# Moving a constants table behind the split rows, so that they begin at another offset within 512 bytes

## What is computed

```
# block 1: Fourier and convolution mixer, then 16 experts, each taking 32 tokens
h  = modulate(rms_norm(x));  p = h @ w_in                      # 1024 -> 5632
y_a = real(fft2(u_f)) @ w_fourier;  y_b = (b_g * conv3(c_g * v)) @ w_conv_out
x  = x + gate * ((sig(g_a) * y_a + sig(g_b) * y_b) @ w_o)
x  = x + gate * sum_over_experts(vals * (silu(xe @ w_gate) * (xe @ w_up)) @ w_down)
# block 2: two kinds of attention side by side
proj = rms_norm(x) @ w_in_2;  o_a = nsa_attention(...);  o_b = moba_attention(...)
x  = x + rms_norm((sig(.) * (o_a @ w_a) + sig(.) * (o_b @ w_b)) @ w_o)
# block 3: two layers, four kinds of attention and a gated feed-forward part
for l in 0, 1:
    proj = rms_norm(x) @ w_in_3[l];  x = x + concat(four attentions) @ w_o_3[l]
    h = rms_norm(x);  x = x + (silu(h @ w_gate) * (h @ w_up)) @ w_down
out = rms_norm(x)
```

## The kernel before

| tile | before | after |
|---|---|---|
| ring, x | 0 | 0 |
| cst | 0 | 256 |
| vec1 | 64 | 0 |
| vec2 | 0 | 448 |
| stat | 320 | 320 |
| xR | 320 | 256 |
| mt2, arena | 320 | 320 |

## Time and profile before

### The profile page before, as it was taken

How to read it: one execution, slowest core, us unless ns; L and a number is a source line. 1 busy time by engine, 2 the same in 40 slices (tenths; PEclk the granted TensorE clock), 3 DMA queues, 4 the chain that set the end, 5 groups by cost and what they waited for, 6 DMA issues and landing times.

```text
span 2136.2 us, 32653 instructions
## 1 busy us (share of the span) xinstructions
PE 1709.5 (80%) x13430; PEld 1239.9 (58%) x13430; DVE 808.7 (38%) x1592; ACT 646.8 (30%) x1144; POOL 84.0 (4%) x143
## 2 busy tenths in 40 slices
PE   5999966566556566665665799988999999999998
PEld 3899921112111222111121699988989988989996
DVE  2374621001110111110011557775656654666654
ACT  3334310000000000000000347655644334655333
POOL 2000010000000000000000200101100001000000
PEclk8999987877888787878778799999989999999999
DMA  9996799999999999999999753407065535145640
GB/s 368 328 323 231 284 380 428 429 428 428 428 430 428 428 429 428 428 428 430 428 428 430 274 187 120 139 33 269 21 213 182 196 138 184 40 159 170 195 178 20
DMA packets 152995, 613.51 MB, mean 287 GB/s; under 512 B 8816, under 2 KB 62138, under 8 KB 128312
## 3 DMA queue, kind: packets, MB, share of 16 engines
q1 hardware_dynamic: 148928, 604.47, 71.9%
q0 software_dynamic: 3200, 7.14, 1.1%
q10 hardware_dynamic: 760, 0.39, 0.1%
HBM read 610.88 MB, written 5.03 MB: 288 GB/s over the span
## 4 chain that ended last, share of the span: by engine, by line
PE 54%; DMA 38%; DVE 3%; ACT 2%; issue 1%; SPq 1%; DVEq 1%; POOL 0%; POOLq 0%; ACTq 0%
PE psum L1472 52%; DMA ring<-in_w_down_e 19%; DMA ring<-in_w_up_e 18%; DMA ring<-in_w_in 1%; PE psum L1842 1%; DVE ring_r L703 1%; SPq L749 0%; ACT arena L1069 0%; ACT ring_r L694 0%; PE psum L1577 0%; POOL stat L944 0%; SPq L768 0%; DVE arena L2447 0%; PE psum L2006 0%; PE psum L1991 0%
## 5 line engine op out<-in xcount | busy, mean ns | idle before, releaser
L1472 PE MATMUL psum<-ring,arena 128*32 128x512 f32 (+2 forms) x4314 | 532.7, 638 | 282.0 <-DMA ring<-in_w_up_e 129.6
L1472 PE MATMUL psum<-xR_r,ring_r 128*128 128x256 f32 x4416 | 553.0, 283 | 2.1 <-DVE xR_r L2086 1.3
L1472 PEld LDWEIGHTS psum<-xR_r,ring_r 128*128 128x128 f32 x4416 | 531.1, 189 | 12.7 <-issue 10.8
L1472 PEld LDWEIGHTS psum<-ring,arena 128*32 128x32 f32 x4314 | 153.9, 133 | 628.0 <-DMA ring<-in_w_up_e 209.4
L703 DVE TENSOR_TENSOR ring_r<-ring,ring_r 128x1024 fp32r<-128x1024 f32 (+2 forms) x332 | 377.9, 1172 | 195.9 <-ACT ring_r L694 195.2
L694 ACT CAST ring_r<-ring 128x1024 fp32r<-128x1024 f32 (+2 forms) x332 | 320.2, 1007 | 392.1 <-PE psum L1472 373.9
L1472 PE MATMUL psum<-arena 128*128 128x256 f32 (+7 forms) x1270 | 191.2, 382 | 20.1 <-DVE arena L2322 9.9
L2319 DVE TENSOR_TENSOR arena<-arena,psum 128x512 f32<-128x512 f32 x16 | 16.9, 1055 | 478.8 <-PE psum L1472 478.8
L1472 PE MATMUL psum<-ring_r,xR_r 128*128 128x256 f32 (+3 forms) x1344 | 171.5, 284 | 9.5 <-DVE xR_r L2071 6.0
L1472 PE MATMUL psum<-ring_r,arena_r 128*128 128x512 f32 (+1 forms) x912 | 170.8, 348 | 2.2 <-DVE mt L2698 2.2
L1472 PEld LDWEIGHTS psum<-ring_r,xR_r 128*128 128x128 f32 x1344 | 161.4, 191 | 12.2 <-DVE ring_r L703 6.3
(11 more groups left out here) (270 smaller groups left out, 957.8 us busy)
## 6 DMA issues: line engine op xcount, KB each, us to landing
ring<-in_w_gate_e SPq DMA_DIRECT2D x64, 2048.0 KB, 25.8
ring<-in_w_down_e SPq DMA_DIRECT2D x63, 2048.0 KB, 26.4
ring<-in_w_up_e SPq DMA_DIRECT2D x62, 2048.0 KB, 24.9
ring<-in_w_in SPq DMA_DIRECT2D x30, 2048.0 KB, 12.5
ring<-in_w_ada SPq DMA_DIRECT2D x12, 2048.0 KB, 14.6
ring<-in_w_gate SPq DMA_DIRECT2D x22, 1024.0 KB, 5.5
ring<-in_w_up SPq DMA_DIRECT2D x22, 1024.0 KB, 8.1
ring<-in_w_down SPq DMA_DIRECT2D x10, 2048.0 KB, 7.8
```

The lines of the kernel that those rows point to most:

```text
L1472: return nc.tensor.matmul(o, l, r, start=s, stop=e)
```

## The change

Two allocations are moved: `cst` now comes behind `xR`, and so does `stat`. No instruction is added, taken away or reordered. `xR` moves from 320 to 256 bytes beyond a multiple of 512 (from the ring's start), `cst` from 0 to 256, `vec1` and `vec2` as in the table above; `stat` moves by whole multiples of 512, and `mt2`, `arena` and everything in them stay where they were.

```diff
         ring, ring_r = twice("ring", RINGM * SLOT)
         x = sb("x", TT * D).rearrange("p (t d) -> p t d", t=TT)
 
-        cst = sb("cst", a["c_kept"].shape[1])
         vec1 = sb("vec1", 112)
         vec2 = sb("vec2", 78)
-        stat = sb("stat", 512)
         x_moe, xR = twice("xR", 2 * KT * T)
         xR = xR.rearrange("p (c k t) -> p c k t", c=2, k=KT)
+        cst = sb("cst", a["c_kept"].shape[1])
+        stat = sb("stat", 512)
         mt2 = sb("mt2", 2 * 512)
         arena, arena_r = twice("arena", ARENA)
```

## The result

The changed kernel took 2153.0 us, the median of 4 runs (2152.3 to 2153.2); the kernel before took 2138.4 us beside it (4 runs, 2136.9 to 2141.3). The ratio is 1.0069 (95% interval 1.0053 to 1.0084): **slower by 14.6 us**. The forecast of 2131 us had the wrong sign, and 2153 lies above its range of 2110 to 2148. The profiled execution took 2152.28 us with a span of 2149.6, which is 13.4 us more than the span before.

A forecast was written before the change was run, and what follows sets the result against it. PE's pace outside the experts was taken to bound the kernel; -10.2 us for moving `xR_r` and +1.1 for block 1 made -9.1, from 2137.99 to 2128.9, plus 1.9 to the runs' median: 2131 us, range 2110 to 2148.

The forecast's parts named there:

- What bounds the kernel, and what the change touches: Outside the experts PE's pace sets the time nearly one for one; 4416 moving and 1152 stationary `xR_r` matmuls are touched.
- `cst` at nothing: Moving `cst` from 0 to 256, read by DVE and PE's transposes, was taken as 0, with 2 us on each end.
- g, not the operand that moves, decides: In split matmuls, pace goes with g, stationary offset less moving one, modulo 512: 118.7, 117.8 or 113.3 ns.
- The pace at g = 256: Both `xR_r` groups were put at 115.5 ns, midway between settled paces: -10.2 us for moving, 0 for stationary.
- rival 3: Places within 128 bytes matter, so `xR_r` products join the slow 118.7 ns: +7.7 us, 2147 us; chance 0.26.
- the sign of being wrong that the prediction had named: A feed-forward part settling at one pace in both layers would refute the forecast, moving the result by 4 to 5 us.
- no pattern worse than any seen: Range's upper end, 2148 us: rival 3 plus 1 to 2 us of the identity, leaving out any worse pattern.
- The gain or loss in block 1: Block 1 makes 960 of 4416 moving matmuls, 2.2 us of gain; waits for weights take back half, +1.1 us.
- the bound of 110.9 ns: Lower pace limit from weight loads in a 152-column piece: -30.5 us for moving `xR_r`, -5.3 us for stationary.
- Rival 2: Pace depends on how a stretch begins, not on g, so moving `xR_r` stays as it is: 2140 us; chance 0.27.
- The isolated gap of 109.2 ns: Skill formula for 256 columns; reaching it would give the moving group -38 us, an estimate not used in the sum.

The follow-up runs named there:

- the small kernel: Separate kernel computing nothing of the reference: stretches of 48 split matmuls, moving or stationary tile shifted; 113.3 to 120.0 ns at multiples of 64 bytes.
- combination (192, 192, 128): Byte shifts of moving high, moving low, stationary low against stationary high; whole kernel with `xR` at 64, weights' high halves moved: 2126.7 us against 2136.1 for the kernel before.

## Why the prediction was wrong

**What bounds the kernel, and what the change touches: right.** PE's pace in the products with `xR` passed into the time nearly one for one, no wait came or went, and the Fourier and convolution stretches, whose operands stayed, kept 118.7 and 117.8. `cst` at nothing agrees with the run (0.4 us slower, ratio 1.0005), whose interval of -3 to +5 us is wider than the 2 us I put on each end.

**g, not the operand that moves, decides: right**, and now shown by shifting either, or both, with one limit: at some g there are two paces, and g does not say which.

**The pace at g = 256: this step failed, and it made the wrong sign.** I took g modulo 512, saw 118.7 at 128, 117.8 at 192 and a mixture at 320, and went on along that line to 115.5 at 256. The function has the period 256: 320 is 64, and 256 is 0, a value that the trace before did not hold at all. The rows could not show the period, since no two of their values were 256 apart; they could show that nothing was known at 0, and the interpolation hid that. With the period left open, the class of 256 was unknown, and rival 3 would have stood at least level with the forecast. Both feed-forward parts settled at one pace, 120.0 ns, which is the sign of being wrong that the prediction had named.

**Rival 3 had the direction, but neither the rule nor the size.** A multiple of 128 joined the slow side. Its rule, that the places within 128 bytes matter, would make 0 and 128 alike, and 64 and 192; the paces of both pairs differ, and the period is 256. I gave it the pace of the Fourier pieces, 118.7 (4.0 us moving, 3.7 us stationary), where 120.0 was measured: 9.3 us and 4.3 us. The Fourier pieces are g = 128, which is a class of its own; at 384, where g is 128, the whole kernel gave 2147.2, the very figure of rival 3, and at 256 it gave 2153. The bound "no pattern worse than any seen" was set by the worst row, with nothing that said it was the worst possible: that is why 2153 lies outside the range.

**The gain or loss in block 1: wrong.** I let the DMA take back half of it. On the chain, the delay is 3.7 us when block 1's last pieces begin (239.00 before, 242.73 after), 4.3 us at the first expert's matmuls (279.43 and 283.71) and still 3.3 us at the start of block 2. Of the 3.7 us, 0.45 were there before block 1's first matmul; the 3.3 that its products made arrive at block 2. So nearly all of it passes through the experts, whose stream is all DMA, as far as one pair of traces can tell: the time from block 1's last pieces to block 2 ranges from 959.0 to 962.3 us over the nine traces of whole kernels. The working also left out that block 1 makes 288 of the 1152 stationary matmuls. And the bound of 110.9 ns has one short first step of 74 ns in it; once running, that piece goes at 111.6, so the lower bound for the moving group should have been -27 and not -30.5 us. Nothing came near it.

**Rival 2, and the page that spoke for it.** The Trainium skill (SBUF - State Buffer, Who interferes with whom) gives PE two read ports of its own and lets it wait for nobody. Whatever the ports are, with the same instructions the runs show 113.3 ns at one difference and 120.0 at another. The measurement decides: where the two operands lie to each other changes the pace. Rival 2 was right in one half: with `xR` at 448 two feed-forward parts with the same g ran at 113.5 and 117.9, so something at the start of a stretch does pick between two paces. The isolated gap of 109.2 ns for 256 columns that the Trainium skill's formula gives (TensorE: Matmul & The Clock Gate, Back-to-back issue gap) was reached at none of the shifts tried; the best was 113.3.

**What stays open.** Which unit the two streams meet in; why at several of the differences there are two paces and what picks one when a stretch begins. Two paces explain a part of the spread of the runs (each feed-forward part is worth 4.5 us, and the kernel before ranged from 2129 to 2143 us), but not all: with `xR` at 0, where the products with `xR` showed no second pace, four runs still spread over 5.8 us. A part of that lies in layer 2 between the two feed-forward parts, which took 220.4 to 223.2 us over the nine traces; why was not looked into.

## What to carry to other kernels

Where PE runs back to back and loads weights for every matmul, the difference of the two operands' offsets in SBUF was worth up to 6% of its pace here (113.3 to 120.0 ns), so any change in the order or size of even a small allocation ahead of them can move the time. When a parameter's effect is known at a few values only, ask first what its period is and whether the new value is inside a class that has been seen; a point between two neighbours is no estimate. A stretch of 48 matmuls for each shift costs 6 us of device time and gives the whole map. The map gave 0.3% here by the order of the allocations alone, and 0.5% with one of them 128 bytes shorter.

## What the runs showed of the hardware

- 256-column float32r matmuls, each with its own full weight load: 120.0 ns with both operands at the same offset modulo 256 bytes, 118.7 or 120.0 at 128, 113.3 or 117.8 at 64 and at 192 (stationary less moving; in the small kernel 64 mostly the first, 192 mostly the second), 116.6 to 120.1 at the odd multiples of 32.
- A stretch settles at its pace within some ten matmuls and holds it to its end, for 1008 matmuls in a feed-forward part: 114.54 and 119.00 us in one execution.
- With the high and low halves of the weights 128 bytes apart (combination (192, 192, 128)) the slow pace was not seen in the one trace taken: 26 of 26 long stretches at 113.3 to 113.8.
- With 512 columns the range is 226.7 to 234.3 ns. With loads of 32 columns a stretch of 48 took 5.63 to 5.65 us at a moving shift of 192 (g = 64, the good one of the full load too), and 5.64, 5.94 and 5.78 at 64. With loads of 64 columns the paces are 113.3 ns at 0, 116.7 at moving shifts of 64 and 128 and 119.0 at 192.
